# Normed activations placed 64 bytes further from the weight buffers, the arena of the other activations kept at 64 modulo 128 bytes

## Time and profile before

| | |
|---|---|
| profiled execution | 2256.7 us; span 2255.0 us; mean granted clock 0.984 |
| the three timed runs | 2254.41, 2258.55, 2258.77 us |
| TensorE | 2177.2 us busy (97%), 17596 matmuls |
| VectorE | 1302.1 us (58%) |
| ScalarE | 1188.7 us (53%) |
| GpSimd | 255.6 us (11%) |
| DMA | 392 MB in the queues of SyncE and ScalarE, mean 175 GB/s |
| chain that ended last | TensorE 62%, issue 18%, VectorE 9%, ScalarE 6% |

### The profile page before, as it was taken

The page is one execution under the profiler, slowest core; times in us unless marked ns, Lnnn a source line. Parts: engine busy times, 40 slices in busy tenths (PEclk is TensorE's granted clock), DMA queues, the critical chain, the costliest instruction groups (busy, mean ns, idle before and its releaser), DMA issues.

```text
span 2255.0 us, 46586 instructions
## 1 busy us (share of the span) xinstructions
PE 2177.2 (97%) x17596; PEld 2134.9 (95%) x17596; DVE 1302.1 (58%) x1641; ACT 1188.7 (53%) x1565; POOL 255.6 (11%) x325
## 2 busy tenths in 40 slices
PE   6999999999999999999999999999999979999996
PEld 5999999999999999999999999999998969999996
DVE  5555654444456666666665555556665465756544
ACT  5444445545446656666665454644554444555542
POOL 2000000000110000000001111000100123111111
PEclk7999999999999999999999999999999999999998
DMA  3445445555555544545546555445444433444453
GB/s 148 170 171 181 167 167 187 186 186 186 182 191 187 186 178 175 186 168 185 186 170 218 208 209 219 169 170 185 169 166 170 177 138 132 169 149 149 149 183 114
DMA packets 54927, 393.83 MB, mean 175 GB/s; under 512 B 6097, under 2 KB 6225, under 8 KB 7522
## 3 DMA queue, kind: packets, MB, share of 16 engines
q1 hardware_dynamic: 54432, 392.19, 48.6%
q10 hardware_dynamic: 450, 1.02, 0.1%
HBM read 391.09 MB, written 2.10 MB: 174 GB/s over the span
## 4 chain that ended last, share of the span: by engine, by line
PE 62%; issue 18%; DVE 9%; ACT 6%; POOL 3%; DVEq 1%; ACTq 1%; DMA 0%; POOLq 0%
PE acc L552 18%; PE acc L554 17%; PE acc L553 17%; ACT w_hi L919 4%; DVE w_lo L1324 3%; PE tok L594 2%; PE tok L595 2%; PE tok L596 2%; DVE f_pre L1549 1%; ACT L1095 1%; DVE f_val L1560 1%; DVE f_val L1556 1%; DVE f_act L1569 1%; POOL sumsq_g L1892 1%; PE att L612 1%
## 5 line engine op out<-in xcount | busy, mean ns | idle before, releaser
L1324 DVE TENSOR_TENSOR w_lo<-raw,w_hi 128x1024 fp32r<-128x1024 f32 x740 | 904.9, 1236 | 802.7 <-ACT w_hi L919 801.0
L552 PE MATMUL acc<-n_hi,w_hi 128*128 128x256 f32 x3488 | 999.9, 287 | 26.6 <-POOL n_lo L1901 19.0
L554 PE MATMUL acc<-n_hi,w_lo 128*128 128x256 f32 x3488 | 991.6, 284 | 0.0
L553 PE MATMUL acc<-n_lo,w_hi 128*128 128x256 f32 x3488 | 991.5, 284 | 0.0
L919 ACT ACTIVATE w_hi<-raw 128x1024 fp32r<-128x1024 f32 x740 | 760.2, 1052 | 385.3 <-PE acc L554 167.8
L552 PEld LDWEIGHTS acc<-n_hi,w_hi 128*128 128x128 f32 x3488 | 673.9, 193 | 32.5 <-issue 23.4
L553 PEld LDWEIGHTS acc<-n_lo,w_hi 128*128 128x128 f32 x3488 | 674.2, 193 | 0.5
L554 PEld LDWEIGHTS acc<-n_hi,w_lo 128*128 128x128 f32 x3488 | 674.1, 193 | 0.0
L552 PE MATMUL acc<-f_hi,w_hi 128*128 128x256 f32 x688 | 189.9, 276 | 0.0
L553 PE MATMUL acc<-f_lo,w_hi 128*128 128x256 f32 x688 | 189.9, 276 | 0.0
L554 PE MATMUL acc<-f_hi,w_lo 128*128 128x256 f32 x688 | 189.9, 276 | 0.0
(11 more groups left out here) (313 smaller groups left out, 2980.6 us busy)
## 6 DMA issues: line engine op xcount, KB each, us to landing
raw<-stream_in SPq DMA_DIRECT2D x370, 1024.0 KB, 4.8
x<-x_in SPq DMA_DIRECT2D x4, 512.0 KB, 7.3
out<-x SPq DMA_DIRECT2D x4, 512.0 KB, 2.7
v_bias<-v_bias_in ACTq DMA_DIRECT2D x1, 512.0 KB, 8.8
par<-params_in ACTq DMA_DIRECT2D x1, 287.0 KB, 5.3
pos_i<-positions_in ACTq DMA_DIRECT2D x1, 128.0 KB, 6.7
gk<-gk_in ACTq DMA_DIRECT2D x1, 68.0 KB
```

Of the source, the lines that this page charges most:

```text
L552: nc.tensor.matmul(out, w_hi[:, s, wc], hi[:, k, :], start=first, stop=False)
L553: nc.tensor.matmul(out, w_hi[:, s, wc], lo[:, k, :], start=False, stop=False)
L554: return nc.tensor.matmul(out, w_lo[:, s, wc], hi[:, k, :], start=False, stop=last)
L1324: nc.vector.tensor_tensor(w_lo[:, s, :], raw[:, s, :], w_hi[:, s, :].bitcast(fp32), ALU.subtract).then_inc(lo_ready, 1)
```

## The change

A tensor `apart` of 64 bytes a partition, which nothing reads or writes, is placed between `w_lo` and `n_hi`. `arena_start` is no longer the next multiple of 64 but the next address that is 64 modulo 128. `n_hi`, `n_lo` and all that `sb` places behind them lie 64 bytes further; the arena begins 128 bytes further and keeps its place modulo 128. No instruction changes but for addresses.

```diff
 RING = 4
 FREE = 1
+LINE = 128
...
         w_hi = sb("w_hi", [P, RING, UNIT], fp32r)
         w_lo = sb("w_lo", [P, RING, UNIT], fp32r)
+        apart = sb("apart", [P, 16])
         n_hi = sb("n_hi", [P, KT, T], fp32r)
         n_lo = sb("n_lo", [P, KT, T], fp32r)
...
-        arena_start = -(-nc.sbuf_base // 64) * 64
+        arena_start = -(-(nc.sbuf_base - LINE // 2) // LINE) * LINE + LINE // 2
         arena_end = nc.sbuf_usable_end
```

## The result

The changed kernel is slower. Its median is 2263.11 us (20 runs, 2257.84 to 2266.81) against 2258.43 us of the kernel before (20 runs, 2254.41 to 2261.5): ratio 1.0021, 95% interval 1.0014 to 1.0028, a small difference but clear of no change. I had forecast 2249.8, that is faster. The first rival had said 2263.0, with a chance of 0.25.

The account below looks back on a forecast made before the run. TensorE, busy 97% of the span, was taken as the bound, except in wup. Terms summed to -4.7 us, with -4.1 for short streams -8.8, giving a median of 2249.8 us; likeliest range 2244 to 2254, whole range 2221 to 2264.

Parts of the forecast that it names:

- The first rival: Rival 1: every break at full clock ends in 353, wdown's too; sum +4.5 us, 2263.0, chance 0.25.
- address and history set the pitch: TensorE threes: 360 ns at equal residue; at 64 bytes apart 340 or 353, settled by the last break.
- The fourth rival: No effect: n's pitch comes from something else than the residue; 2258.5, chance 0.10.
- nothing in wup: wup: 1376 threes get faster but double rounds stay at 23.38 us; zero.
- The ring of VectorE and ScalarE: wup: the two engines wait only for each other, 23.38 us per double round, hiding TensorE's gain.
- mix, merge with wout, gla, latent and mla: Terms: mix -4.3 and -0.9; merge zero, wout +3.4; gla -3.1 and +2.6; latent, krope and mla -2.4 us.
- the quarter below: Short streams with many breaks: a quarter of 1232 threes at 340, 13.3 ns each; -4.1 us.
- I take 340: zero: wdown: 688 threes stay at 340 after wup's last accumulator wait; zero, other end +9.2 us.
- glaout: The og stream, at 113.4 ns before, got no term in the sum.

Follow-up runs that it names:

- the break in the kernel before: Kernel before with one float32 product of 128 columns put between wup and wdown: 2266.13 us, ratio 1.0045.
- the bridge in the changed kernel: Changed kernel with 12 added fp32r products of equal residue, result unused, ahead of wdown (such a group is a bridge): 2256.75 us, ratio 1.0000.
- the three experiments on residues: Kernel before with all at one residue, 2288.89 us; changed kernel with n 32 and arena 96 bytes past the weights, 2265.21 us, and the reverse, 2272.95 us.
- its bridge versions: Changed kernel with added equal-residue products ahead of wdown, 2256.75 us; merge and wdown, 2257.93; or four places, 2257.24, 2263.19, 2241.99 and 2260.62 us.
- the four later ones: Changed kernel with equal-residue products at four places: 12 each, 2257.24 us; 5 each, 2263.19; float32 product and 10 (6 at mlaout), 2241.99; 24 (6 at mlaout), 2260.62.
- the first three runs: Float32 product before wdown in the kernel before, 2266.13 us; 12 equal-residue products in the changed kernel ahead of wdown, 2256.75 us, and ahead of merge and wdown, 2257.93 us.
- the 5-product run: Changed kernel with 5 equal-residue products ahead of merge, ahead of wdown, behind wdown's first pass and ahead of mlaout: 2263.19 us, ratio 1.0028.
- two bridges: Changed kernel with 12 equal-residue products ahead of merge and 12 ahead of wdown: 2257.93 us, ratio 0.9994.

## Why the prediction was wrong

**Held: address and history set the pitch.** At equal residue 360, at 64 apart 340 or 353, settled at the last break. The run with everything at one residue shows the first, the break in the kernel before and the bridge in the changed kernel show the second, one from each side. The fourth rival is excluded: 31 us hung on addresses alone. The rule that stood behind it (the Trainium skill, "SBUF — State Buffer", section "Who interferes with whom": TensorE's two read ports are independent of one another) is not borne out as the whole truth by these runs, 120.0 against 113.3 ns.

**Held: nothing in wup.** 499.7 us for 500.0 with n at 117.7 instead of 120.0, and 498.9 with a sixth of the matmuls left out. The ring of VectorE and ScalarE is the bound of this stage, which has 39% of the n threes.

**Held in the main: mix, merge with wout, gla, latent and mla, apart from the quarter below.** Expected -5.2, +3.4, -0.5, and -2.4 for the last two together; measured -5.7, +3.6, -0.6, -1.4. The last is little more than half of what was expected.

**Failed: "I take 340: zero" for wdown.** This step decided the sign. I had one stream that began after a wait for its accumulator, c at 1934.79 in the earlier trace rows, and it ran at 340; I took that as a property of the kind of wait. In the changed kernel every one of the 17 long stretches of n in wup begins with such a wait, and all 17 run at 353. f follows the last of them without a break and is at 353 too. In its place stands this: f is at 340 where a stream of equal residue runs into it (the kernel before, and all five profiles with 10 or more such products ahead of wdown), and a break at full clock mostly leads to 353 (as the break in the kernel before shows for f). The price of the step was right, 688 x 13.3 = 9.2 us, measured 9.2.

The kind of wait does not fix the pitch. The break that I had read, c behind a wait of 1.4 to 1.6 us for VectorE's `kn`, stands in 11 profiles with the arena 64 bytes apart (all but those of the three experiments on residues). c goes on at 113.3 or 113.4 ns in 5 of them, the kernel before and the changed one included, and at 117.8 in 6. One of these is the first run with a bridge:

```profile
1933.09 0.38 PE L554 MATMUL acc<-c_hi,w_hi 128*128 128x256 f32 x1 [1.38 <-DVE kn L1827]
```

And in wup, in the seven profiles with n 64 bytes apart from the weights (the changed kernel and its bridge versions), 12 of the 121 waits of this kind led to 340, all in the four later ones, and each of the 12 was back at 353 after 96 matmuls. So the rows before showed one of two outcomes of that break. And as the last wait in wup stands 192 matmuls ahead of f, none of the 121 would have carried 340 into wdown.

**Failed: "a quarter" of the small streams at 340, -4.1 us.** It came from the same sample of four kinds. Counted in the starts of the records of five profiles (the kernel before, the changed one and the first three runs), in streams at 64 apart: of 222 breaks 207 lead to 353 and 15 to 340, 12 of these behind the transposes of the latent attention and 3 at c, with 1.7 to 1.9 us between the starts. That is one in fifteen, all in streams of 16 threes. Later profiles have more of them, as the 12 in wup show.

**Missing: glaout, +3.2 us in the profile.** I gave og nothing because it was at 340 before, after a spell at half clock. It is at 353 after, though that profile has the spell as well. The run with six products ahead of mlaout shows it at 353 with n where it was before, but without the spell; the 5-product run shows it at 340 with n moved. With the spell the kernel before and its two variants were at 340 three times, the changed kernel and its one variant at 353 twice. That is too few to say whether these 3.2 us belong to the change. If not, they are part of why the profiles are 8.0 us apart and the medians 4.7.

**The choice between cases.** With rival 1 the sum was +4.5 us, and the medians differ by 4.7. That it comes so near is in part luck: the stages of the two profiles add up to 8.1, with glaout in no sum. The evidence for this rival was in the same rows as the forecast: the mo stream of 256 threes and the c tiles of three rounds against one stretch of 4.8 us. I weighed a likeness of kind (a wait for an accumulator) above the count. And with gains possible only in stages where TensorE is the bound, the losses in wout and wdown (944 threes) could not be made up at 353.

**Where the expected gain of the 64 bytes is.** At 340 it exists: the version with float32 products ahead of its bridges runs 21 us faster than the changed kernel and 16 faster than the one before, by one float32 product and 10 more at each of three places and 6 at a fourth. Without them, putting n apart takes away the very streams of equal residue that brought hm, yc, mg and f to 340.

## What to carry to other kernels

Read the pitch of matmuls (time over count, in windows in which TensorE never waits) for each pair of operand buffers, not the duration in the groups; a few per cent between tensors with the same form point to their addresses, and a difference between stretches of one tensor to what stands before them. Before moving a buffer, ask which streams are fast only because of the stream that TensorE runs right ahead of them. And ask in each stage whether TensorE is its bound: two engines that wait only for each other set the pace however busy TensorE looks.

One stretch of a kind is not a rule for the kind: here the same break went both ways in profiles of kernels that are alike at that place. When the sign of a forecast hangs on it, the forecast should sit between the cases.

## What the runs showed of the hardware that was not expected

- A stream of fp32r products of 256 columns, weights and streamed operand 64 bytes apart modulo 128, has two lasting pitches at full clock, 113.3 and 117.8 ns, on the same instructions and addresses. It kept the lower for 3096 matmuls in a row (merge and wout with two bridges) and the higher for 3287 (mix's last tiles to the end of wout in the changed kernel).
- At equal residue it is 120.0 ns. From a steady 120.0 a stream that goes on without a break at 64 bytes apart went to 113.3 wherever it was seen: at hm in each pass of merge, at f, at the first og tiles of the kernel before.
- Of the 20 bridges in the profiles 14 led to 113.3; the 6 others (12 and 24 products ahead of merge, 5 ahead of merge and twice in wdown, 6 ahead of mlaout once) left 117.8 behind them. None of these 6 had reached a steady 120, but neither had 3 of the 14. Straight out of a stream at 117.8, 5 of 7 with 12 or 24 products worked and 0 of 3 with 5; behind a float32 product, 7 of 8 with 5 to 12. The last two came out of a stream at 113.3.
- At equal residue there is a second pattern, 121, 120, 124, 118, 117 ns, which averages 120 and lasted for 24 products. It was seen in two bridges, and 117.8 followed both.
- 32 and 96 bytes apart gave 116.6 to 120.0 ns.
- A break with 0.19 us between two starts instead of 0.11, early in wdown, cost some 8 us by estimate: 1805 matmuls at 117.8 instead of 113.3.

Open: what in the chip holds the two pitches, why a steady 120 leads to the lower one, and what decides at a break. That a float32 product makes a bridge surer is likely, not shown: six executions are few (two of them, at 2248, were 6 us slower than the other four), and no run had the float32 product without the bridge at these places in the changed kernel.
